# Banded key ring with four slots, and the merge stage's first loads issued inside sparse attention

## The reference

```python
# first block: two attentions o_a (MLA, 8 heads) and o_b (sparse, 8 heads, 2 key heads), both 512 wide
o_a = mla_attention(q_a, k_a, v_a) * silu(gate_a)
o_b = dsa_attention(q_b, k_b, v_b, q_i, k_i, w_i, 256) * silu(gate_b)
merged = (sigmoid(m_a + b_merge[0]) * (o_a @ w_branch_mla)
          + sigmoid(m_b + b_merge[1]) * (o_b @ w_branch_dsa))
x = x + merged @ w_out
# second block: banded attention, 16 heads, 4 key heads of 64, window 128, T5 bias and a sink per head
q, k, v, z = split(rms_norm(x) @ a_w_in)
s = q @ k.T / 8 + bias          # each block of 128 queries reads its own and the preceding block of keys
p = softmax([s, sink])[:-1]
x = x + ((p @ v) * silu(z)) @ a_w_out
return rms_norm(x)
```

## Time and profile before

| | |
|---|---|
| median of 3 executions | 3423.64 us (3419.33 to 3426.46) |
| profiled execution | 3424.3 us, span 3422.5 us |
| PE / weight loads / DVE / ACT / POOL busy | 93 / 78 / 61 / 53 / 23 % of the span |
| mean granted PE clock | 0.964 of full |
| sparse attention | about 1614 to 2081 us of the span |
| merge | 2081 to 2489 us |
| banded attention | 2489 to 3045 us |
| final | 3045 to 3422 us |

### The profile page before, as it was taken

How to read it: one execution, slowest core, us unless ns; L and a number is a source line. 1 busy time by engine, 2 the same in 40 slices (tenths; PEclk the granted TensorE clock), 3 DMA queues, 4 the chain that set the end, 5 groups by cost and what they waited for, 6 DMA issues and landing times. The chain is left out here.

```text
span 3422.5 us, 51529 instructions
## 1 busy us (share of the span) xinstructions
PE 3171.4 (93%) x17464; PEld 2665.5 (78%) x17464; DVE 2079.6 (61%) x5117; ACT 1820.8 (53%) x3608; POOL 775.1 (23%) x1078
## 2 busy tenths in 40 slices
PE   7999879999989999996899995999989999969998
PEld 5888668888768777775677775999878888869997
DVE  5766768888746756653899885434446666632112
ACT  5565557777656666653777773111246666632121
POOL 5444401011101112231211001100034444311110
PEclk9999989999999999998999997999999999969999
DMA  5666654336152222225211104544441221144332
GB/s 170 201 205 195 198 131 107 76 69 141 58 202 81 71 82 80 81 86 127 60 40 42 31 7 152 172 147 134 145 136 55 73 73 53 55 136 138 123 124 74
DMA packets 307189, 370.47 MB, mean 108 GB/s; under 512 B 24800, under 2 KB 251936, under 8 KB 303088
## 3 DMA queue, kind: packets, MB, share of 16 engines
q1 hardware_dynamic: 293728, 320.77, 32.4%
q0 software_dynamic: 13200, 46.42, 4.2%
HBM read 216.32 MB, written 150.80 MB: 107 GB/s over the span
## 5 line engine op out<-in xcount | busy, mean ns | idle before, releaser
L93 PE MATMUL i_p_g<-i_hT_lo,i_wh 128*128 128x512 f32 x768 | 308.5, 402 | 9.3 <-DVE i_wl L1632 9.3
L94 PE MATMUL i_p_g<-i_hT_hi,i_wl 128*128 128x512 f32 x768 | 306.6, 399 | 0.0
L95 PE MATMUL i_p_g<-i_hT_hi,i_wh 128*128 128x512 f32 x768 | 306.5, 399 | 0.0
L1650 DVE SCALAR_TENSOR_TENSOR i_score<-i_relu,i_w,i_score 128x1024 f32<-128x1024 f32 (+7 forms) x154 | 155.1, 1024 | 168.4 <-ACT i_relu L1534 166.5
L1544 ACT ACTIVATE i_above<-i_score,i_less 128x2048 bf16<-128x2048 f32 (+13 forms) x140 | 183.2, 1308 | 106.6 <-POOL i_less L1601 69.6
L1081 DVE TENSOR_TENSOR mla_tl<-mla_p_t,mla_th 128x512 fp32r<-128x512 f32 (+1 forms) x320 | 186.1, 606 | 45.3 <-ACT mla_th L1124 41.6
L1124 ACT ACTIVATE mla_th<-mla_p_t 128x512 fp32r<-128x512 f32 (+1 forms) x320 | 163.9, 530 | 86.3 <-PE mla_p_t L1021 83.6
L1081 DVE TENSOR_TENSOR dsa_tl<-dsa_p_t,dsa_th 128x512 fp32r<-128x512 f32 x272 | 179.9, 686 | 39.8 <-ACT dsa_th L1124 33.7
L1051 DVE CUSTOM_DVE_ANT_0 dsa_probs<-dsa_p_s,dsa_mask 128x512 f32<-128x512 f32 (+3 forms) x320 | 184.6, 605 | 25.4 <-PE dsa_p_s L1790 23.8
L1124 ACT ACTIVATE dsa_th<-dsa_p_t 128x512 fp32r<-128x512 f32 x272 | 155.2, 593 | 67.3 <-PE dsa_p_t L1021 66.4
L1021 PE MATMUL mla_p_t<-ident,mla_probs 128*128 128x128 f32 x1088 | 172.7, 274 | 11.1 <-DVE mla_tl L1081 9.7
(11 more groups left out here) (340 smaller groups left out, 9768.8 us busy)
## 6 DMA issues: line engine op xcount, KB each, us to landing
scratch_gates<-i_ob SPq DMA_DIRECT2D x96, 256.0 KB, 2.4
m_m<-scratch_gates SPq DMA_DIRECT2D x64, 256.0 KB, 4.6
f_hs<-scratch_h2T SPq DMA_DIRECT2D x16, 1024.0 KB, 10.0
scratch_qkT<-b_th SPq DMA_DIRECT2D x64, 192.0 KB, 2.5
scratch_qkT<-b_tl SPq DMA_DIRECT2D x64, 192.0 KB, 2.9
i_ws<-in_w_in SPq DMA_DIRECT2D x24, 512.0 KB, 4.5
b_xt<-in_x SPq DMA_DIRECT2D x16, 512.0 KB, 4.8
scratch_h<-b_xh POOLq DMA_DIRECT2D x16, 512.0 KB, 3.0
```

The lines of the kernel that those rows point to most:

```text
L93: pe.matmul(out, l[0], r[1], start=start, stop=False)
L94: pe.matmul(out, l[1], r[0], start=False, stop=False)
L95: return pe.matmul(out, l[0], r[0], start=False, stop=stop)
L1650: nc.vector.scalar_tensor_tensor(out=acc, in0=r, scalar=w[:, t, h:h + 1], in1=acc, op0=ALU.mult, op1=ALU.add).then_inc(summed, 1)
```

## The change

Two edits stand together.

**Banded stage.** `kh` and `kl` get a fourth slot. The keys of tiles t with t % 3 == 0 are written to slot 0 and, from t = 3 on, to slot 3 as well: ACT makes two copies and DVE two subtractions for these tiles. The scores of such a tile read slots 2 and 3, all other tiles t-1 and t as before, so every tile but tile 0 takes two matmuls of 256 columns per head. Room for it comes from `kd`, which now lies in the first half of `qs` (so chunk 0's evacuation waits for query transposes, chunk 1's for the key transposes), and from `lower`, which has one buffer in place of two and waits for the join of the unit before.

**Merge.** The tiles `o`, `gate`, `x` and `junk` are placed above the space that sparse attention uses, in an object `MergeInputs`. When SP in sparse attention is at unit 8 it waits for the stores of units 0 to 3 and issues weight tile 0, o and gate of both y of group 0, and weight tiles 1 and 2, seven DMAs of 512 KB. The merge stage starts with the first two `m` pairs, then weight tile 3, the o of group 1, weight tile 4 and so on. The other tiles of the merge stage move to other offsets.

```diff
+    def sync_unit(self, sp, n):                      # class Dsa
+        if n == 4 * KV:
+            for p in range(2):
+                sp.wait_ge(self.sems["stored"][p], 16 * KV)
+            self.merge_in.load_first(sp)
...
-        kd = sb("kd", [P, WKV, 2, HD])
         qs = sb("qs", [P, 2, KD, P], F32R)
         qT = sb("qT", [P, WH, P], F32R)
-        kh = sb("kh", [P, WKV, 3, P], F32R)
-        kl = sb("kl", [P, WKV, 3, P], F32R)
+        kd = qs[:, 0, 0:WKV].bitcast(F32).rearrange("p g (a d) -> p g a d", a=2)
+        kh = sb("kh", [P, WKV, 4, P], F32R)
+        kl = sb("kl", [P, WKV, 4, P], F32R)
...
-        lower = sb("lower", [P, 2, GT])
+        lower = sb("lower", [P, GT])
...
+        slots_of = lambda t: ([3] if t >= 3 else []) + [0] if t % 3 == 0 else [t % 3]
...
-                tiles = [t % 3] if t == 0 else [(t - 1) % 3, t % 3]
+                keys, slots = (slice(P, 2 * P), slice(0, 1)) if t == 0 else (
+                    slice(0, 2 * P), slice((t - 1) % 3, (t - 1) % 3 + 2))
...
-                        q, out = qT[:, 4 * g + x], p_s[:, half, x % 2]
-                        if len(tiles) == 2 and tiles[1]:
-                            nc.tensor.matmul(out, q, kh[:, g, tiles[0]:tiles[1] + 1], start=True, stop=False)
-                            last = nc.tensor.matmul(out, q, kl[:, g, tiles[0]:tiles[1] + 1], start=False, stop=True)
-                            continue
-                        for y, slot in enumerate(reversed(tiles)):
-                            part = out[:, P - y * P:2 * P - y * P]
-                            nc.tensor.matmul(part, q, kh[:, g, slot], start=True, stop=False)
-                            last = nc.tensor.matmul(part, q, kl[:, g, slot], start=False, stop=True)
+                        q, out = qT[:, 4 * g + x], p_s[:, half, x % 2, keys]
+                        nc.tensor.matmul(out, q, kh[:, g, slots], start=True, stop=False)
+                        last = nc.tensor.matmul(out, q, kl[:, g, slots], start=False, stop=True)
...
                 if ch == 0:
                     if t >= 1:
-                        is_turned(act, ("K", t - 1, 0))
+                        is_turned(act, ("Q", t - 1, 1))
...
-                if t >= 1:
-                    is_turned(act, ("Q", t - 1, 2 * ch - 1))
+                if ch == 1:
+                    is_turned(act, ("K", t, 0))
+                elif t >= 1:
+                    is_turned(act, ("Q", t - 1, 3))
...
-                    nc.scalar.activation(kh[:, :, t % 3], src, ACT.Copy).then_inc(k_hi, 1)
+                    for slot in slots_of(t):
+                        last = nc.scalar.activation(kh[:, :, slot], src, ACT.Copy)
+                    last.then_inc(k_hi, 1)
...
-                if u >= 2:
-                    act.wait_ge(out_done, u - 1)
-                nc.scalar.activation(lower[0:HD, u % 2], p_o[HD:P], ACT.Copy).then_inc(lowered, 1)
+                if u >= 1:
+                    act.wait_ge(out_done, u)
+                nc.scalar.activation(lower[0:HD], p_o[HD:P], ACT.Copy).then_inc(lowered, 1)
...
-                    nc.vector.tensor_tensor(kl[:, :, t % 3], src, kh[:, :, t % 3].bitcast(F32),
-                                            ALU.subtract).then_inc(done, 1)
+                    for slot in slots_of(t):
+                        last = nc.vector.tensor_tensor(kl[:, :, slot], src, kh[:, :, slot].bitcast(F32), ALU.subtract)
+                    last.then_inc(done, 1)
...
+class MergeInputs:
+    def __init__(self, nc, at, oaT, obT, gates, w_branch):
+        self.o, self.gate = (nc.alloc_sbuf_tensor_at(f"m_{n}", [P, 2, 4, 2 * P], F32, offset=at + 8192 * x)
+                             for x, n in enumerate(("o", "gate")))
+        self.x = nc.alloc_sbuf_tensor_at("m_x", [P, 2, D], F32, offset=at + 16384)
+        self.junk = nc.alloc_sbuf_tensor_at("m_junk", [P, D], F32, offset=at + 24576)
+        self.raw = [self.x[:, 0], self.x[:, 1], self.junk[:]]
+    def load_first(self, sp):
+        self.load_branch(sp, 0)
+        for y in range(2):
+            self.load_o(sp, 0, y)
+        for n in range(1, len(self.raw)):
+            self.load_branch(sp, n)
...
-            load_w(0)
-            load_o(0)
             load_m(0)
-            for n in range(1, KD):
+            load_m(1)
+            for n in range(slots, KD):
                 load_w(n)
-                if n == 3:
-                    load_m(1)
+                if n == slots:
                     load_o(1)
```

More of the change, by code:

```diff
@@ L1984, in stage_banded @@
         last_slot, late = 12 * NT + 2, CHUNKS - 1
-        raw = [probs[:, x].rearrange("p h k -> p (h k)") for x in range(3)] + [
-            x[:].rearrange("p a n -> p (a n)") for x in (ot, lower)]
+        raw = [probs[:, x].rearrange("p h k -> p (h k)") for x in range(3)] + [ot[:].rearrange("p a n -> p (a n)")]
         raw_of = lambda k: raw[k // 2][:, k % 2 * GT:(k % 2 + 1) * GT]
         tile_of = lambda u: u // WKV
+        slots_of = lambda t: ([3] if t >= 3 else []) + [0] if t % 3 == 0 else [t % 3]
         first_key = lambda u: P if tile_of(u) == 0 else 0
@@ L2356, in join @@
                     dve.wait_ge(stored[u % 2], 16 * (u // 2))
-                nc.vector.tensor_tensor(ot[0:HD, u % 2], p_o[0:HD], lower[0:HD, u % 2], ALU.add).then_inc(out_done, 1)
+                nc.vector.tensor_tensor(ot[0:HD, u % 2], p_o[0:HD], lower[0:HD], ALU.add).then_inc(out_done, 1)
             for use in (("X", 0, 0), ("X", 0, 1)):
@@ L2419, in load_x, with load_o, load_branch, stage_merge @@
         sp.dma_start(self.xt[:, t % 2], self.x1[t * P:(t + 1) * P, :]).then_inc(self.x_in[t % 2], 16)
-def stage_merge(nc, sem, oaT, obT, gates, w_branch, w_out, residual, out, rs, at, band):
+class MergeInputs:
+    def __init__(self, nc, at, oaT, obT, gates, w_branch):
+        self.sources, self.gates, self.w_branch = (oaT, obT), gates, w_branch
+        self.o, self.gate = (nc.alloc_sbuf_tensor_at(f"m_{n}", [P, 2, 4, 2 * P], F32, offset=at + 8192 * x)
[3 more added lines that the diff above has]
+        self.raw = [self.x[:, 0], self.x[:, 1], self.junk[:]]
+        self.o_in = [nc.alloc_semaphore(name=f"m_o_in{x}") for x in range(2)]
+        self.w_in = [nc.alloc_semaphore(name=f"m_w_in{x}") for x in range(2 * KD)]
+    def load_o(self, sp, g, y):
+        at = slice(g * 2 * P, (g + 1) * 2 * P)
+        sp.dma_start(self.o[:, y], self.sources[y].rearrange("(k p) t -> p k t", p=P)[:, :, at])\
+            .then_inc(self.o_in[y], 16)
+        sp.dma_start(self.gate[:, y], self.gates[y * 512:(y + 1) * 512].rearrange("(k p) t -> p k t", p=P)[:, :, at])\
+            .then_inc(self.o_in[y], 16)
+    def load_branch(self, sp, n):
+        sp.dma_start(self.raw[n % len(self.raw)], self.w_branch[n]).then_inc(self.w_in[n], 16)
+    def load_first(self, sp):
[4 more added lines that the diff above has]
+            self.load_branch(sp, n)
+def stage_merge(nc, sem, given, gates, w_out, residual, out, rs, at, band):
     GO = 2 * P
@@ L2433, in stage_merge @@
     with ExitStack() as c:
-        space = Space(nc, (at, nc.sbuf_usable_end))
+        space = Space(nc, (at, at + 5 * BAND_W), (at + 6 * BAND_W, at + 11 * BAND_W), (at + 5 * BAND_W, at + 6 * BAND_W),
+                      (at + 11 * BAND_W + 28672, nc.sbuf_usable_end))
+        o, gate, x, junk, raw, o_in, w_in = (given.o, given.gate, given.x, given.junk, given.raw, given.o_in,
+                                             given.w_in)
         sb = lambda n, s, d=F32: space(f"m_{n}", s, d)
@@ L2437, in stage_merge @@
         bl = sb("bl", [P, KD, 2, KO, P], F32R)
-        o = sb("o", [P, 2, KO, GO])
-        gate = sb("gate", [P, 2, KO, GO])
         oh = sb("oh", [P, 2, KO, GO], F32R)
@@ L2452, in stage_merge @@
         p_y = c.enter_context(nc.psum_tensor("m_p_y", [P, 2, 2, GT], F32))
-        w_in = sem("m_w_in", 2 * KD)
         n_band = 2 * KD // 2
         band_in, band_hi, band_lo = sem("m_band_in", n_band), sem("m_band_hi"), sem("m_band_lo")
-        o_in, m_in, x_in, stored = (sem(f"m_{n}", 2) for n in ("o_in", "m_in", "x_in", "stored"))
+        m_in, x_in, stored = (sem(f"m_{n}", 2) for n in ("m_in", "x_in", "stored"))
         (w_hi, w_lo, gated, o_hi, o_lo, branched, weighed, summed, a_hi, a_lo, filled, added, squared, meaned,
@@ L2463, in stage_merge @@
         tok = lambda g: slice(g * GO, (g + 1) * GO)
-        raw = [x[:, 0], x[:, 1], junk[:]]
         slots = len(raw)
@@ L2479, in load_w @@
                     sp.wait_ge(w_lo, n - slots + 1)
-                src = w_branch[n] if n < KD else w_out[rows(n - KD), :]
-                sp.dma_start(raw[n % slots], src).then_inc(w_in[n], 16)
+                if n < KD:
+                    given.load_branch(sp, n)
+                else:
+                    sp.dma_start(raw[n % slots], w_out[rows(n - KD), :]).then_inc(w_in[n], 16)
             def load_o(g):
-                for y, src in enumerate((oaT, obT)):
-                    if g >= 1:
-                        sp.wait_ge(o_lo, 2 * g - 1 + y)
```

(10 more changed lines are left out.)

10 lines of the change are left out of this document (6 added, 4 removed).

## The result

The changed kernel takes 3399.38 us (median of 4 executions, 3396.45 to 3407.41) against 3424.69 for the kernel before on the same chip: ratio 0.9933, interval 0.9918 to 0.9948, 22.9 us (17.8 to 28.1). Forecast were 3401.4 us and a gain of 22.2. The profiled execution took 3407.41 us around a span of 3405.6, the longest of the four.

What follows compares the result with a forecast made beforehand. PE was taken to bound the banded stage, and a load-and-split chain the merge opening. Gains of 6.5 (merge), 13.3 (scores) and 2.4 (tile 15) sum to 22.2, so 3423.64 becomes 3401.4 us; range 3395 to 3411.

Steps and rivals of the forecast that it cites:

- Steady tiles: Banded stage, tiles 3, 6, 9, 12: wide score matmuls save 0.83 us per unit, 13.3 for 16 units, bounds 12.6 to 13.8.
- Merge opening, size: Start of merge: PE's first matmul 4.9 us earlier, 6.5 us gained with the first groups of matmuls, bounds 4.9 to 7.2.
- the term on the clock: Merge opening: PE rises to 2.4 GHz at 2094.5 to 2096.6, so f=1 ends 6.9 or 6.0 us earlier.
- Merge opening, POOL: Merge opening: POOL's second split follows right behind the first, 2.34 us each, so PE's second wait is gone.
- Early loads: Sparse attention, unit 8: seven DMAs (3.5 MB) moved there cost 0, bounds 0 and 3.5 us.
- Tail: Banded stage, tile 15: unit 60 saves 0.8 and unit 61 1.6, together 2.4 us, bounds 0.8 and 3.5.
- Rival 3: Banded stage: the new wait for key transposes lands on the path, net 16 us slower, 3440; chance 2%.
- the copies: Banded stage: writing keys twice on ACT and DVE fits in idle time, cost 0; uncovered, 3.0 us.
- the ring: Banded stage's four-slot keys: 13.3 us forecast from trace rows; an estimated 0.4 us by the skill's isolated-gap formula.

Runs made afterwards that it cites:

- narrow: The kernel after, with every score product of tiles 1 to 15 cut into 128-column matmuls: 3446.42 us, ratio 1.0068.
- before_again: The kernel before, unchanged, run for a second profile: 3423.59 us, ratio 1.0001.
- ring_only: The kernel before with the edits of the banded stage alone: 3407.99 us, ratio 0.9957 to the kernel before.
- merge_only: The kernel before with the merge edits and early loads alone, banded stage as before: 3415.65 us, ratio 0.9978 to the kernel before.
- after_again: The kernel after, unchanged, run for a second profile: 3399.04 us, ratio 0.9937 to the kernel before.
- m_first: The kernel after, with SP issuing m pairs 2 to 7 ahead of weight tiles 8 to 13 in merge, not behind: 3399.04 us, ratio 0.9924 to the kernel before.
- tail_and_m: The kernel after with m_first's order, plus two final-stage loads moved behind the stores of units 59 and 61: 3393.95 us, ratio 0.9909 to the kernel before.

## Why the prediction was right

**Steady tiles.** 13.3 us forecast for 16 units, 13.3 measured from tile 3 to tile 15. The step that carried it, to read the price of a matmul from the distance of two starts in the same stream, is confirmed by `narrow`.

**Merge opening, size.** From PE's last sparse matmul to its first merge matmul the profile of after shows 4.9 us less than that of before (18.6 to 13.7), as worked out; against before_again and ring_only it is 4.5. With the stage itself it is 414.1 to 414.3 us in the three profiles with the old opening, 407.3 to 407.4 in after and merge_only and 404.9 in after_again, so this part brought 6.7 to 7.0 or 9.2 to 9.4 us where 6.5 was said with bounds 4.9 to 7.2. The upper bound was too low: the term on the clock was mis-sized. I put the rise to 2.4 GHz at 5.8 to 7.9 us behind PE's first matmul. It came 6.2 us behind it in the kernel after and 3.5 behind it in after_again. Of the 2.5 us between the two merge stages this makes 1.2; the pause before f=6 makes 0.3, and the rest lies in the stretches at 1.2 GHz behind the two later pauses, which the forecast gave no gain. Timeline of after_again, PE, the first matmul of the stage, and the last at 1.2 GHz with the first at 2.4:

```profile
2083.84 0.55 PE L93 MATMUL m_p_b<-m_ol,m_bh 128*128 128x256 f32 x1 [13.27 <-POOL m_ol L2690]
...
2087.07 0.38 PE L93 MATMUL m_p_b<-m_ol,m_bh 128*128 128x256 f32 x1 [0.33 <-POOL m_ol L2690]
2087.29 0.28 PE L94 MATMUL m_p_b<-m_oh,m_bl 128*128 128x256 f32 x1
```

In the three profiles with the merge opening of before it came 8.1 to 8.7 us behind it; in the ten with the new one, in two groups, at 3.4 to 3.6 or at 5.9 to 6.2. The five of the second group all had a sparse attention of 463.3 to 464.4 us, the five of the first one of 459.6 to 461.9. With SP's order of the kernel after, merge is 391.2 us in the first group (two profiles) and 393.6 to 393.7 in the second (three). Between after and after_again these two make 5.8 us; another 8.2 of the 14.2 by which their profiled times differ lie ahead of sparse attention. Why a long sparse attention and a late rise go together stays open.

**Merge opening, POOL.** I let both splits take 2.34 us each. They took 5.67 together, a microsecond more, and PE's second wait was therefore not gone but 0.32 us. The trace of before has such a pair back to back, at the start of group 1, and it took as long there:

```profile
2134.10 5.67 POOL L2656 TENSOR_TENSOR m_ol<-m_o,m_oh 128x1024 fp32r<-128x1024 f32 x2 [36.10 <-ACT m_oh L2602]
```

That row was the one to take for two splits in succession. The microsecond lies in the second split alone. Timeline of the kernel after, POOL and DVE, each as one instruction:

```profile
2095.16 3.35 POOL L2690 TENSOR_TENSOR m_ol<-m_o,m_oh 128x1024 fp32r<-128x1024 f32 x1
...
2094.88 1.40 DVE L2698 TENSOR_TENSOR m_bl<-m_x,m_bh 128x1024 fp32r<-128x1024 f32 x1 [2.07 <-ACT m_bh L2629]
```

DVE begins its subtraction of the next weights 0.28 us before POOL's second split, and that split ends 2.23 us behind DVE's end, about the length that it has singly. In the kernel before the order was the other one: POOL's first split had begun when DVE gated y=1, POOL took its 2.34, and it was DVE's instruction that was long, 2.80 us where the gating of y=0 took 1.23:

```profile
2091.67 2.80 DVE L2669 TENSOR_TENSOR m_o<-m_o,m_gate 128x1024 f32<-128x1024 f32 x1 [1.79 <-DMA m_gate<-scratch_gates]
```

In both the instruction that begins second seems to wait for the other to end. No run moved one of the two to try it.

**Early loads.** Cost 0 forecast and 0 found, in after_again for the stage and in after for units 8 to 12.

**Tail.** 2.4 us were forecast, 0.8 for unit 60 and 1.6 for unit 61. From the scores of unit 60 to the first matmul of the final stage the profile of before shows 62.6 us and that of after 59.5, 3.1 less. But the 1.6 rests on a chance of one execution. In before_again and in merge_only, which have the same narrow tile 15, the clock fell later. The timeline of before_again, the first and the last score matmul of unit 61:

```profile
2991.92 0.22 PE L2145 MATMUL win_p_s<-win_kh,win_qT 128*128 128x128 f32 x1
...
2993.54 0.28 PE L2146 MATMUL win_p_s<-win_kl,win_qT 128*128 128x128 f32 x1
```

1.62 us for the 16, where the profile of before has 3.1 between the same two (and 3.3 up to the next operation); the 8 wide ones of after, at 1.2 GHz, took 1.49. The stretch from unit 60 to the final stage took 60.2 and 60.8 us in these two, and 60.5 and 60.7 in after_again and ring_only: no difference. Unit 60's 0.8 went too. The projections are over there, PE waited for DVE behind unit 60 and waits longer now, 1.79 us for 1.35, which takes back half of it, and unit 61's scores follow 6.4 us (after) and 6.5 (after_again) behind unit 60's where it was 6.7 (before) and 6.6 (before_again). So the tail term was mis-sized, 2.4 for about 0 in most of the profiles. It was made good by the merge term, which came out larger than said, and that the sum of 22.2 lies so near to 22.9 is in part luck.

**Rival 3 and the copies.** The steady tiles show no wait that was not there, so both came out at 0, as said.

**Slips of the working.** By the Trainium skill's formula for the isolated gap the ring would gain an estimated 0.3 us in all and not 0.4 (16 units of 4 heads, 5 ns each). The range ends at 3411, a little under the sum's own bound of 3411.8 and without the spread above it. Neither changes the outcome.

## What to carry to other kernels

In a stage where PE never waits, the distance between the starts of neighbouring matmuls prices an edit well: here 13.3 us forecast and 13.3 measured. Where PE does wait, and at the clock's edges, one profiled execution is one draw: price such a term from two profiles, or widen its bounds by the other clock level over the whole stretch. The same holds for experiments: compare profiles in which the clock rose at the same place, or the difference may be that of the clock. A late load may gain little by a slightly earlier issue; ahead of three more 512 KB loads, the wait for it was gone.

## What the runs showed of the hardware

- A matmul of 128 columns in a stream of different stationary tiles costs nearly as much as one of 256: 0.111 us from start to start against 0.119, at 2.4 GHz. At 1.2 GHz both cost 0.21 (16 narrow ones 3.31 us in before, 8 wide ones 1.71 in after, unit 61).
- In five of the ten profiles with the early loads the granted clock fell to 1.2 GHz inside unit 6 or 7 of sparse attention, or in both, in code that ran at 2.4 GHz in the others. In after each drop cost 1.6 us.
- The same 256 KB loads took 4.3 us from issue to landing (after), each right behind one 512 KB load. With a 512 KB load and another pair issued within 3 us behind them they took 5.6 in one profile (m_first) and 4.4 in another of the same order (tail_and_m).
- POOL's subtraction of 128x1024 took 2.34 us singly, and 5.67 for two in succession, of which the second had 3.35. It began while DVE was at a subtraction; that this is the cause was not tried.
